# Bias rows stored sixteen times in memory, each copy shifted by one number more, and read back at multiples of 64 bytes

## The chip, the cores and the metric

The kernel runs on one core of one Trainium2 chip (trn2). The metric is device time in microseconds (us) of one execution. Before the change three runs took 1264.16 us in the median (1261.74 to 1264.27).

## What is computed

One inference step of a two-layer decoder for a prompt of 256 tokens and 8 samples of one token each (model width 1024, 16 heads of 64). Layer 0 is attention in three groups g, with windows 128, 512, 2048 and dilations 1, 4, 16; layer 1 is a pooling mixer; each is followed by a mixture of experts (16 experts, two per token). Everything is float32. What matters for the change is the relative bias of the prompt's attention:

```
step = BAND + qi - kj                               # distance of query and key
bias = bias_tab[t5_bucket(max(step, 0) * dilation)] # (query, key, head)
sc = q . k * HEAD_DIM ** -0.5 + bias
sc = where(step in window, sc, -1e30); p = softmax(sc)
```

The bias depends on the distance alone. So for a head and a group it is one row of numbers by distance, and the 128 queries of a block need that row at 128 successive offsets. The three groups are merged by a softmax over their log sums, and attention also hands back keys and values; the caches of the samples are copied to the outputs, shifted by one token (168 copies of 1 MB, called `move` in the code).

## The kernel before, in words

The five instruction streams (PE, DVE, ACT, POOL, SP) are written out by hand and meet at semaphores. SP issues nearly all large DMAs, in one fixed order on one queue (q1): weights and caches for the matmuls, with copies of the sample caches (`move`, L342) put between them as filling. ACT's own DMAs go to a second queue (q10), POOL's to a third (q0). All queues are served by the same 16 DMA engines.

**Start.** x is transposed on PE (L1035), its squares are summed (L287), and ACT takes the root (L294). At the same time PE makes the bias rows: a table of 33 x 48 numbers times 0/1 rows by distance (L1041) gives 16 heads x 384 distances for each group, and DVE copies them to `bias_rows` on 16 partitions (L771). ACT then stores them to the tensor `bias_by_distance` in HBM (L612), issues six DMAs for constants (L613 to L618), and waits until the store has landed (L619), because the memory of `bias_rows` is used again in the next stage. SP, which has issued three chunks of w_qkv (2 MB each) and five copies of the first cache, waits for the same store (L352) and then issues seven more copies. POOL waits for it ahead of its first broadcast (L483).

**w_qkv.** 72 tiles of 128 columns: PE multiplies (L1059), ACT squares the result (L626), PE sums squares (L1066), ACT takes the root (L632), DVE its reciprocal and the product (L787, L788), POOL keeps the tile (L492). PE runs at most two tiles ahead of the first square. SP loads chunks of four tiles into three slots; the chunk for tiles 12 to 15 is issued when four tiles are done.

**Samples.** The samples' attention over the caches: scores on DVE beside the tiles, then PE's products with V (L1103, L1110, L1103), whose V loads come in two halves of three loads of 2 MB (L376). Ahead of the second half SP issues the bias loads of heads 0 to 3 (`bias_load`, L367), and five copies.

**Prompt attention.** 16 heads, one step per head. PE makes the scores (L1127, L1130), DVE adds the bias from `bias_t` and takes the maximum (L846, L849, L851), ACT takes exponentials (L670, L672), DVE scales (L862, L863), PE transposes (L1138) and multiplies with V (L1145, L1150). `bias_t` has four slots of 128 x 3 x 256 numbers; when head h has been biased (`biased`), SP loads the slot for head h + 4 (L367) and issues one copy. A load is one DMA: partition p reads, for each group, 256 numbers from the row of its head beginning at number p, so its 384 pieces of 1 KB begin at multiples of 4 bytes.

After that come w_o (L1171), two mixtures of experts with the pooling layer between them, and the transposes of the result.

Of the kernel before, what the change touches and what calls it, by code (L numbers as in the profile page):

```python
# [7 lines left out]
F32 = mybir.dt.float32  # L8
# [4 lines left out]
P = 128  # L13
# [30 lines left out]
def build(nc, x_prompt, x_sample, cache_w128, cache_w512, cache_w2048, state_pool, w_qkv, q_norm,  # L44
# [4 lines left out]
    _, SEQ, D = x_prompt.shape  # L49
# [3 lines left out]
    G = len(WINDOWS)  # L53
    NB, GH = rel_bias.shape
    H = GH // G
# [10 lines left out]
    BV = 3 * P  # L66
# [13 lines left out]


    qkvs_dram = nc.dram_tensor("qkv_of_samples", [NS, 3, G, D], F32, kind="Internal").ap()
    bias_dram = nc.dram_tensor("bias_by_distance", [H, G, BV], F32, kind="Internal").ap()

    with ExitStack() as ctx:
        def sb(name, shape):
# [61 lines left out]
        bias_rows = cut(7680, (G, BV))  # L148
# [176 lines left out]
        def _(sp):  # L325
# [23 lines left out]
            sp.wait_ge(buckets_landed, 32)  # L349
            for b in range(5):  # L350
                move(0, b, 0)
            sp.wait_ge(bias_stored, 16)  # L352
            for b in range(5, NS):
                move(0, b, 0)
            for n in range(PIECES[1]):
# [8 lines left out]

            def bias_load(h, b):

                sp.dma_start(bias_t[:, b], bass.AP(tensor=bias_dram.tensor, offset=h * (G * BV),  # L367
                                                   ap=[[1, P], [BV, G], [1, SEQ]])).then_inc(bias_landed[b], 16)

            for half in range(2):  # L370
                for g in range(G):
# [97 lines left out]
        def _(pool):  # L469
            pool.dma_start(pool_s[0, :, 0:STATE - 1, :].rearrange("b s c -> b (s c)"),  # L470
                           state_pool[0, :, 1:STATE, :].rearrange("b s c -> b (s c)")).then_inc(tokens_sent, 16)
            for g in range(G):
                def load_k(b):
                    pool.dma_start(slot(3)[:, b % 4 * D:(b % 4 + 1) * D], k_strided[g][b]).then_inc(k_landed[b % 4], 16)

                def spread_q(b):
                    at = 32 * (b // 3 + 1)

                    if b % 2 == 0 and b <= 2:
                        pool.wait_ge(zn_kept, g * NQK + (NQK - 2 + b))  # L480
                    if b >= 1:
                        pool.wait_ge(q_spread, g * NS + b)
                    pool.wait_ge(bias_stored, 16)  # L483
                    nc.gpsimd.partition_broadcast(q_rep[b % 2][:, :], q_row[at:at + 1, b % 3, :], channels=P).then_inc(q_spread, 1)  # L484

                for b in range(4):
                    load_k(b)
                for n in range(NQK):
                    pool.wait_ge(zn_ready, g * NZ + n + 1)
                    if n == KT + 6:  # L490
                        pool.wait_ge(q_spread, g * NS + 2)
                    nc.gpsimd.tensor_copy(qk[:, g, n // KT, n % KT, :], zn[:, n % 4, :]).then_inc(zn_kept, 1)  # L492
                    if n == KT + 3:
                        pool.wait_ge(z_stored, g * NZ + KT)
                        for at in range(0, NS, 3):
                            n_rows = min(3, NS - at)
                            pool.dma_start(q_row[32 * (at // 3 + 1):32 * (at // 3 + 1) + 1, 0:n_rows, :],
                                           qkv_s[at:at + n_rows, 0, :]).then_inc(q_rows_landed, 16)
                        pool.dma_start(qkvs_dram[:, 0, g], qkv_s[0:NS, 0, :]).then_inc(q_sent, 16)
                    if n == KT + 5:  # L500
                        pool.wait_ge(q_rows_landed, g * 48 + 48)
                        for b in range(2):
                            spread_q(b)
                for b in range(NS):
                    pool.wait_ge(scored, g * NS + b + 1)
                    if b + 2 < NS:
                        spread_q(b + 2)
                    if b + 4 < NS:
                        load_k(b + 4)
                pool.wait_ge(z_stored, (g + 1) * NZ)  # L510
                pool.dma_start(qkvs_dram[:, 1:3, g], qkv_s[0:NS, 1:3, :]).then_inc(rows_sent, 16)
                dst = kv_p[g][0, 0].rearrange("t w h e -> t w (h e)")
                if g == 0:
                    pool.dma_start(dst[:, 0, :], k_tok[1]).then_inc(tokens_sent, 16)
                    for a in range(2):
                        pool.dma_start(dst[a * HD:(a + 1) * HD, 1, :], v_tok[a * HD:(a + 1) * HD, 1, g, :]).then_inc(tokens_sent, 16)
                else:
                    for b in range(2):
                        pool.dma_start(dst[b * P:(b + 1) * P, 0, :], k_tok[b]).then_inc(tokens_sent, 16)
                    pool.dma_start(dst[:, 1, :].rearrange("(b p) c -> p b c", p=P), v_tok[:, :, g, :]).then_inc(tokens_sent, 16)  # L520
                pool.wait_ge(rows_sent, g * 16 + 16)
                pool.dma_start(kv_s[g][0, :, kv_s[g].shape[2] - 1].rearrange("b w h e -> b w (h e)"),
                               qkv_s[0:NS, 1:3, :]).then_inc(tokens_sent, 16)
# [73 lines left out]
        def _(ac):  # L597
            dma = ac.dma_start
# [10 lines left out]
            ac.wait_ge(setup_done, 1)  # L609
            norm_root(ac, 0, h_filled, KT)  # L610
            ac.wait_ge(bias_copied, 1)
            dma(bias_dram.rearrange("h g d -> h g d"), bias_rows[0:H, :, :]).then_inc(bias_stored, 16)  # L612
            dma(bucket_s[:], c_bucket_sample.rearrange("g n k -> n g k")).then_inc(consts_landed, 16)  # L613
            dma(same_batch[:], c_same_batch).then_inc(consts_landed, 16)
            dma(rank[:], c_rank[:, 0:NE]).then_inc(consts_landed, 16)
            dma(slot_no[:], c_rank[:, NE:NE + CAP]).then_inc(consts_landed, 16)
            dma(same_head[:], c_rank[:, NE + CAP:]).then_inc(consts_landed, 16)
            dma(tri[:], c_tri).then_inc(consts_landed, 16)  # L618
            ac.wait_ge(bias_stored, 16)  # L619


            with ac.Fori(0, G) as g:
# [124 lines left out]
        def _(dve):  # L747
# [90 lines left out]
            def step(i, s, live, behind):  # L838
                h = i * 4 + s
                b = s % 2  # L840
                if live:
                    dve.wait_ge(scores_ready, h + 1)
                    dve.wait_ge(bias_landed[s], i * 16 + 16)
                    c = 8 * b
                    vec.memset(small[:, 60:61], 0.0)
                    vec.tensor_tensor_reduce(out=probs[:, b, 0:G * P].rearrange("p (g k) -> p g k", g=G), in0=bank[0][:, 0:G * P].rearrange("p (g k) -> p g k", g=G),  # L846
                                             in1=bias_t[:, s, :, P:], scale=1.0, scalar=NEG, op0=ALU.add, op1=ALU.max,
                                             accum_out=small[:, 16 + c:17 + c])
                    vec.tensor_tensor_reduce(out=probs[:, b, 3 * P:7 * P], in0=bank[1][:, :], in1=bias_t[:, s, 0:2, :].rearrange("p g k -> p (g k)"),  # L849
                                             scale=1.0, scalar=NEG, op0=ALU.add, op1=ALU.max, accum_out=small[:, 17 + c:18 + c])  # L850
                    chain(vec.tensor_tensor_reduce(out=probs[:, b, 7 * P:], in0=bank[2][:, 0:SEQ], in1=bias_t[:, s, 2, :],  # L851
                                                   scale=1.0, scalar=NEG, op0=ALU.add, op1=ALU.max, accum_out=small[:, 18 + c:19 + c]))
                    vec.tensor_scalar(small[:, c + 3:c + 4], small[:, 16 + c:17 + c], -1.0, None, ALU.mult)
                    vec.tensor_scalar(small[:, c + 2:c + 3], small[:, 17 + c:18 + c], small[:, 18 + c:19 + c], -1.0,
                                      ALU.max, ALU.mult).then_inc(biased, 1)
# [529 lines left out]
```

## Time and profile before

| | before |
|---|---|
| median of 3 runs | 1264.16 us |
| profiled execution, its own time | 1266.1 us |
| its span, first to last instruction | 1263.9 us |
| mean granted TensorE clock | 0.922 of full |
| PE busy | 1113.8 us (88%) |
| DVE / ACT / POOL busy | 435.8 / 234.0 / 225.0 us |
| DMA packets, bytes | 62930, 462.63 MB, mean 366 GB/s |

The page and the views are of one profiled execution. Times are us from the start of the span, and a duration without a unit is in us. PE is the matmul unit (PEld its weight loads), DVE the vector engine, ACT the scalar engine, POOL the GpSimd; SPq, ACTq and POOLq are instructions that only issue DMAs. In a timeline a row is start, duration, engine, line, operation, out<-in and count; the idle time before it and what ended it stand in brackets. For DMA issues the last number is the time from issue to landing, the median where there are several. PEclk is the clock that TensorE was granted, as a share of 2.4 GHz.

### The profile page before, as it was taken

What the parts mean: (1) busy time and instruction counts of PE and PEld (TensorE: products, weight loads), DVE (VectorE), ACT (ScalarE), POOL (GpSimd) and SP (SyncE); (2) the same over time, 40 slices, a digit from 0 to 9 for tenths busy, and PEclk for the clock granted to TensorE, in tenths of its full rate; (3) what the DMA queues carried; (4) which work ended last, traced back from release to release, by engine and by line L of the source; (5) the groups of instructions that cost most, each with busy time, mean ns of one, the idle gap of its engine ahead of it and who ended that gap; (6) DMA issues with size and microseconds to landing.
All of it is one profiled execution on the core that took longest, in us unless ns stands there. A gap on an engine that the chain in (4) does not pass through costs nothing.

```text
span 1263.9 us, 15314 instructions
## 1 busy us (share of the span) xinstructions
PE 1113.8 (88%) x4993; PEld 671.7 (53%) x4994; DVE 435.8 (34%) x859; ACT 234.0 (19%) x524; POOL 225.0 (18%) x484
## 2 busy tenths in 40 slices
PE   5998799999949899974979999999464999999998
PEld 3887588788822588863424444434343344334444
DVE  3456455845830366223101111111743111111113
ACT  1121122112110134211112122111101112112210
POOL 1014112411420122002122222110001122222210
PEclk9999899999967699985989999999665999999999
DMA  9999999999879998899999999999999899999996
GB/s 374 334 357 372 385 387 343 369 389 388 322 239 384 368 308 288 344 320 326 330 399 429 430 427 413 400 399 394 399 325 322 327 396 397 398 395 396 409 420 241
DMA packets 62930, 462.63 MB, mean 366 GB/s; under 512 B 12112, under 2 KB 20192, under 8 KB 47888
## 3 DMA queue, kind: packets, MB, share of 16 engines
q1 hardware_dynamic: 49136, 440.29, 90.8%
q0 software_dynamic: 5536, 18.88, 4.1%
q10 hardware_dynamic: 8232, 3.13, 1.1%
q8 instruction: 14, 0.23, 0.1%
q14 instruction: 12, 0.10, 0.0%
HBM read 455.19 MB, written 183.41 MB: 505 GB/s over the span
## 4 chain that ended last, share of the span: by engine, by line
PE 56%; DVE 8%; DMA 4%; issue 3%; POOL 1%; ACT 1%; ACTq 1%; POOLq 0%; DVEq 0%; SPq 0%
PE bank L1242 17%; PE bank L1264 8%; PE bank L1220 7%; PE bank L1209 5%; DMA region_a<-in_w_up_dram 3%; PE bank L1171 2%; PE bank L1103 2%; PE bank L1130 1%; PE bank L287 1%; PE bank L1138 1%; PE bank L1150 1%; PE bank L1181 1%; PE bank L1270 1%; PE bank L1110 1%; PE bank L1127 1%
## 5 line engine op out<-in xcount | busy, mean ns | idle before, releaser
L1059 PE MATMUL bank<-uT,ring_lo 128*128 128x264 f32 x1152 | 276.0, 394 | 8.5 <-DVE uT L300 6.0
L1059 PEld LDWEIGHTS bank<-uT,ring_lo 128*128 128x128 f32 x1152 | 219.5, 195 | 49.4 <-issue 9.7
L1242 PE MATMUL bank<-ring_lo,scratch 128*64 128x512 f32 x512 | 114.7, 601 | 16.0 <-DMA ring_lo<-in_w_gate_dram 8.0
L787 DVE RECIPROCAL scratch<-scratch 128x264 f32<-128x264 f32 x48 | 86.5, 1802 | 111.0 <-ACT scratch L632 111.0
L1220 PE MATMUL bank<-scratch 128*128 128x512 f32 (+1 forms) x192 | 99.7, 646 | 18.0 <-POOL scratch L570 18.0
L1264 PE MATMUL bank<-ring_lo,scratch 128*64 128x512 f32 x512 | 113.4, 595 | 1.3 <-issue 1.3
L1242 PE MATMUL bank<-region_a,scratch 128*64 128x512 f32 x512 | 112.7, 592 | 1.4 <-DMA region_a<-in_w_up_dram 1.4
L966 DVE TENSOR_TENSOR scratch<-bank,scratch 128x512 f32<-128x512 f32 x16 | 11.1, 691 | 228.5 <-PE bank L1242 228.5
L1209 PE MATMUL bank<-scratch 128*128 128x264 f32 x288 | 80.1, 404 | 4.4 <-DVE scratch L966 3.4
L555 POOL TENSOR_TENSOR small<-epsc 128x1 f32<-128x1 f32 x83 | 15.6, 193 | 378.7 <-PE bank L1270 359.9
L1242 PEld LDWEIGHTS bank<-ring_lo,scratch 128*64 128x64 f32 x512 | 36.8, 138 | 83.6 <-issue 75.4
L1242 PEld LDWEIGHTS bank<-region_a,scratch 128*64 128x64 f32 x512 | 38.3, 137 | 73.2 <-issue 73.2
L1264 PEld LDWEIGHTS bank<-ring_lo,scratch 128*64 128x64 f32 x512 | 35.8, 137 | 70.4 <-issue 70.4
L1209 PEld LDWEIGHTS bank<-scratch 128*128 128x128 f32 x288 | 49.5, 190 | 41.4 <-issue 25.1
L1220 PEld LDWEIGHTS bank<-scratch 128*128 128x128 f32 (+1 forms) x192 | 32.2, 194 | 72.7 <-issue 54.2
L956 DVE TENSOR_TENSOR hT<-bank,hT 128x264 f32<-128x264 f32 x144 | 60.5, 429 | 26.0 <-PE bank L1209 24.9
L960 DVE COPY scratch<-bank 128x512 f32<-128x512 f32 x16 | 11.1, 691 | 169.0 <-PE bank L1220 169.0
L492 POOL COPY region_a<-scratch 128x264 f32<-128x264 f32 x48 | 24.4, 508 | 193.2 <-DVE scratch L788 192.8
L578 POOL TENSOR_SCALAR scratch<-slot_no,scratch 128x64 f32<-128x64 f32 (+1 forms) x96 | 53.4, 574 | 0.0
L626 ACT ACTIVATE scratch<-bank 128x264 f32<-128x264 f32 x48 | 18.8, 391 | 159.7 <-PE bank L1059 159.7
L798 DVE TENSOR_TENSOR ring_lo<-ring_lo,scratch 128x1024 f32<-128x1024 f32 x24 | 41.7, 1738 | 16.6 <-POOL scratch L484 9.9
L738 ACT ACTIVATE scratch<-bank 128x512 f32<-128x512 f32 x32 | 19.1, 597 | 126.6 <-PE bank L1264 126.6
(224 smaller groups left out, 1242.4 us busy)
## 6 DMA issues: line engine op xcount, KB each, us to landing
out_dram<-in_cache_kv_w_dram SPq DMA_DIRECT2D x128, 1023.5 KB, 18.8
ring_lo<-in_w_gate_dram SPq DMA_DIRECT2D x32, 2048.0 KB, 12.0
region_a<-in_w_up_dram SPq DMA_DIRECT2D x32, 2048.0 KB, 15.2
ring_lo<-in_w_down_dram SPq DMA_DIRECT2D x32, 2048.0 KB, 16.5
ring_lo<-in_w_qkv_dram SPq DMA_DIRECT2D x18, 2048.0 KB, 18.0
out_dram<-in_cache_kv_w_dram SPq DMA_DIRECT2D x32, 1022.0 KB, 35.9
ring_lo<-in_cache_kv_w_dram POOLq DMA_DIRECT2D x24, 512.0 KB, 11.8
ring_lo<-in_cache_kv_w_dram SPq DMA_DIRECT2D x6, 2048.0 KB, 14.7
```

Source lines behind the costliest of these rows:

```text
L492: nc.gpsimd.tensor_copy(qk[:, g, n // KT, n % KT, :], zn[:, n % 4, :]).then_inc(zn_kept, 1)
L578: last = nc.gpsimd.tensor_scalar(pick_gate[0:n, b, at], slot_no[0:n, :], pair_at[0:n, 0, b, e:e + 1], pair_at[0:n, 1, b, e:e + 1], ALU.is_ ...
L787: chain(vec.reciprocal(zri[:, n % 2, :], zr[:, n % 2, :]))
L798: chain(vec.tensor_tensor(k_tile, k_tile, q_rep[b % 2][:, :], ALU.mult))
L956: vec.tensor_tensor(hT[:, m, :], spread_bank[m % 4][:, 0:T], hT[:, m, :], ALU.add).then_inc(spread_added, 1)
L1059: last = mm(z_bank[s % 4][:, 0:T], w[:, k, at:at + P], uT[:, k, :], start=(k == 0), stop=(k == KT - 1))
L1103: last = mm(bank[3 + a][rows, :], p_masked[:, b % 2, g, rows], slot(g)[:, at:at + 512], start=(half == 0 and g == 0 and b % 2 == 0), stop= ...
L1171: last = mm(bank[m % 2][:, 0:T], w[:, f % 4, m * P:(m + 1) * P], oT[:, f, :], start=(f == 0), stop=(f == KT - 1))
L1209: mm(spread_bank[m % 4][:, 0:T], y_pair[:, m * P:(m + 1) * P], place, start=True, stop=True).then_inc(spread, 1)
L1220: last = mm(bank[a][:, :], pick[0:sizes[b], b, :], u_tok[0:sizes[b], b, a * 512:(a + 1) * 512], start=(b == 0), stop=(b == 2))
L1242: last = mm(bank[2 + w][rows, :], u_slots[:, k, rows], weights[e][w][:, k, :], start=(k == 0), stop=(k == KT - 1))
L1264: last = mm(bank[4 + a][rows, :], hid[:, f, rows], weights[e][2][:, f, a * 512:(a + 1) * 512], start=(f == 0), stop=(f == FT - 1))
```

## The change

`bias_by_distance` holds each head's rows 16 times. Copy s begins at distance index s, and a row has 384 - 16 = 368 numbers (1472 bytes, a multiple of 64). The store is 16 DMAs, one per copy, and each wait for it now asks for all 16. A load for one head is three DMAs, one per group: partition p = 16 a + s reads from copy s, beginning at number 16 a, which gives the same 256 numbers as before, from an address that is a multiple of 64 bytes. DVE waits for three landings where it waited for one.

```diff
-    bias_dram = nc.dram_tensor("bias_by_distance", [H, G, BV], F32, kind="Internal").ap()
+    SHIFTS = 16
+    BL = BV - SHIFTS
+    bias_dram = nc.dram_tensor("bias_by_distance", [H, SHIFTS, G, BL], F32, kind="Internal").ap()
...
-            sp.wait_ge(bias_stored, 16)
+            sp.wait_ge(bias_stored, 16 * SHIFTS)
...
-                sp.dma_start(bias_t[:, b], bass.AP(tensor=bias_dram.tensor, offset=h * (G * BV),
-                                                   ap=[[1, P], [BV, G], [1, SEQ]])).then_inc(bias_landed[b], 16)
+                for g in range(G):
+                    sp.dma_start(bias_t[:, b, g, :], bass.AP(tensor=bias_dram.tensor, offset=h * (SHIFTS * G * BL) + g * BL,
+                                                             ap=[[SHIFTS, P // SHIFTS], [G * BL, SHIFTS], [1, SEQ]])).then_inc(bias_landed[b], 16)
...
-                    pool.wait_ge(bias_stored, 16)
+                    pool.wait_ge(bias_stored, 16 * SHIFTS)
...
-            dma(bias_dram.rearrange("h g d -> h g d"), bias_rows[0:H, :, :]).then_inc(bias_stored, 16)
+            for s in range(SHIFTS):
+                dma(bias_dram[:, s], bias_rows[0:H, :, s:s + BL]).then_inc(bias_stored, 16)
...
-            ac.wait_ge(bias_stored, 16)
+            ac.wait_ge(bias_stored, 16 * SHIFTS)
...
-                    dve.wait_ge(bias_landed[s], i * 16 + 16)
+                    dve.wait_ge(bias_landed[s], i * (16 * G) + 16 * G)
```

## Rows read from the trace of the kernel before

**Rows 1.** Page: busy us (share) x instructions; chain by engine.

```profile
PE 1113.8 (88%) x4993; PEld 671.7 (53%) x4994; DVE 435.8 (34%) x859; ACT 234.0 (19%) x524; POOL 225.0 (18%) x484
...
PE 56%; DVE 8%; DMA 4%; issue 3%; POOL 1%; ACT 1%; ACTq 1%; POOLq 0%; DVEq 0%; SPq 0%
```

**Rows 2.** Timeline of PE, 20 to 48 us: start, us, engine line op [idle before].

```profile
30.27 9.95 PE L1059 MATMUL bank<-uT,ring_lo 128*128 128x264 f32 x32 [6.03 <-DVE uT L300]
40.06 0.61 PE L1066 MATMUL bank<-scratch,blockones 128*128 128x264 f32 x2
```

**Rows 3.** Timeline of ACT, 24 to 45 us.

```profile
24.28 0.34 ACTq L612 DMA_DIRECT2D bias_by_distance<-scratch  x1
...
27.15 0.45 ACTq L618 DMA_DIRECT2D tri<-in_c_tri_dram  x1
36.70 0.39 ACT L626 ACTIVATE scratch<-bank 128x264 f32<-128x264 f32 x1 [11.94 <-PE bank L1059]
```

**Rows 4.** DMA issues on ACT's queue: count, KB each, us to landing.

```profile
bias_by_distance<-scratch ACTq DMA_DIRECT2D x1, 72.0 KB, 4.6
...
bucket_s<-in_c_bucket_sample_dram ACTq DMA_DIRECT2D x1, 48.4 KB, 5.8
...
same_batch<-in_c_same_batch_dram ACTq DMA_DIRECT2D x1, 4.0 KB, 9.6
rank<-in_c_rank_dram ACTq DMA_DIRECT2D x1, 8.0 KB, 21.2
```

**Rows 5.** Stretches: us, busy per engine (x), PEclk, DMA share, GB/s.

```profile
24.20:28.20 4.00, 0.04 (x1) 0.00 (x0) 3.31 (x5) 0.48 (x1) 0.00 (x0) 1.00 1.06 390
28.97:35.80 6.83, 5.54 (x13) 4.38 (x14) 1.13 (x4) 0.00 (x0) 0.00 (x0) 0.52 1.05 405
```

**Rows 6.** SP's queue: timeline, and landing of the fifth copy.

```profile
1.73 15.38 SPq L348 DMA_DIRECT2D ring_lo<-in_w_qkv_dram  x3
...
24.34 0.59 SPq L342 DMA_DIRECT2D out_dram<-in_cache_kv_w_dram  x1
...
out_dram<-in_cache_kv_w_dram SPq DMA_DIRECT2D x1, 1016.0 KB, 22.4
```

**Rows 7.** DMA queues, 29.3 to 50 us: packets, MB, share of 16 engines.

```profile
q1 hardware_dynamic: 410, 7.42, 102.7%
q10 hardware_dynamic: 410, 0.05, 1.7%
```

**Rows 8.** Stretches in and after the prompt attention, columns of rows 5.

```profile
447.40:452.80 5.40, 5.40 (x41) 4.59 (x40) 3.90 (x14) 2.10 (x7) 2.95 (x4) 1.00 0.95 322
540.00:549.00 9.00, 9.00 (x42) 7.57 (x40) 0.86 (x2) 0.00 (x0) 0.00 (x0) 1.00 0.74 168
```

**Rows 9.** PE and DVE near 445 us, and DVE's waits from 415 to 520.

```profile
443.86 1.46 PE L1130 MATMUL bank<-scratch 64*128 64x256 f32 x6
...
445.36 0.55 DVE L846 CUSTOM_DVE_ANT_1 scratch<-bank,ring_lo 128x384 f32<-128x384 f32 x1 [2.36 <-issue]
...
DVE scratch L846 <- issue: 14.6, 13, 4.3
```

**Rows 10.** SP's first bias load in the loop; its landing.

```profile
427.90 0.40 SPq L367 DMA_DIRECT2D ring_lo<-bias_by_distance  x1
...
ring_lo<-bias_by_distance SPq DMA_DIRECT2D x1, 384.0 KB, 14.3
```

**Rows 11.** SP and PE around the V loads; packets from 371.5 to 378 us.

```profile
370.53 1.96 SPq L367 DMA_DIRECT2D ring_lo<-bias_by_distance  x4
...
383.27 7.35 SPq L376 DMA_DIRECT2D ring_lo<-in_cache_kv_w_dram  x3
...
ring_lo<-in_cache_kv_w_dram SPq DMA_DIRECT2D x1, 2048.0 KB, 16.9
...
403.86 14.14 PE L1103 MATMUL bank<-ring_lo,scratch 128*32 128x512 f32 x48
...
DMA packets 1615, 2.56 MB, mean 393 GB/s; under 512 B 64, under 2 KB 1600, under 8 KB 1600
```

## The prediction

> **What bounds the kernel now.** I read the page first. PE is busy for 88% of the span, and the chain that ended last is mostly PE [rows 1]; the 16 DMA engines are busy nearly throughout, but a stage is only bound by them where PE waits for a landing. So I looked at the two places that the diff touches, each for what ends last there.
>
> The first is the start. PE turns x and sums squares until 24.2, is idle for 6.03 us, runs the first two tiles of w_qkv from 30.27 (32 records, 9.95 us), and then needs the squares of tile 0 (L626, on ACT) for L1066 at 40.06 [rows 2]. ACT issues the store of the bias rows at 24.28 and six constants, the last at 27.15, then waits for the store, and is next busy at 36.70 with L626, for tile 0's z [rows 3]. The store had landed 4.6 us after its issue, at 28.9 [rows 4]. So ACT could leave its wait up to 40.06 - 0.39 = 39.67 and PE would lose nothing: the store has 10.8 us of slack. Everything behind it, 24 tiles in each of three groups, hangs on this chain.
>
> The second is the prompt attention, 422 to 515, one head in 5.4 us. PE is busy 5.40 of 5.40 us there [rows 8], and DVE's add of the bias starts 0.04 us after the last score matmul (443.86 + 1.46 = 445.32 to 445.36) [rows 9]. DVE's idle time ahead of that line, 14.6 us in 13 pieces, is marked "issue", which could hide a wait for the bias [rows 9]; but the load for head 4 was issued at 427.90 and took 14.3 us, so it was there at 442.2, 3.2 us before it was used [rows 10], and the loads after it have a lead of three heads, 16 us. The reads are not what this stage waits for.
>
> **The change, part by part.**
>
> *The store.* One DMA of 16 rows becomes 16 DMAs of 16 x 3 pieces of 1472 B, 1.13 MB in all. Issues on ACT follow each other at (27.15 - 24.28) / 6 = 0.48 us [rows 3], so 15 more take 15 x 0.48 = 7.2 us, and the last store is issued at 31.5. If it landed as the one of before did, 4.6 us later, the wait would end at 36.1, still 3.6 us inside the slack: cost nothing. The six constants move 7.2 us back, to 34.8; they are used only after all 72 tiles.
>
> But it won't land like that, and the trace shows why. On SP's queue lie five copies of a cache, 1016 KB each in 16 pieces of 65 KB, the fifth issued at 24.34, behind the rest of w_qkv [rows 6]. From 29.3 to 50 SP's queue (q1) ran 410 packets with 7.42 MB and ACT's queue (q10) 410 packets with 0.05 MB [rows 7]: the DMA engines take one packet of each in turn, and a packet of q10 stands behind a copy's piece. The 8 small packets per engine of same_batch and rank landed 9.6 and 21.2 us after issue where bucket_s, ahead of the copies, took 5.8 [rows 4]. rank was issued one place, 0.5 us, behind same_batch, so its 128 rows (8 per engine and a completion) came 12.1 us after same_batch's, which is 1.35 us a packet. The 16 stores are 3 pieces and a completion per engine each, 64 packets. They begin to move at about 28, when the engines are turning to the copies; at 1.35 us a packet 64 would take 86 us. That is no real end, because SP waits for the same semaphore (L352) before it issues copies 6 to 12: behind the fifth copy q1 is empty, and the rest of the stores then run freely. The fifth copy landed 22.4 us after 24.34, at 46.7 [rows 6]. All the stores' bytes at the 390 GB/s of that stretch [rows 5] are 1.13 / 0.39 = 2.9 us, most of it spent ahead of or between the copies on some engines and behind them on others. Bounds for the end of the wait: 36.1 (stores slip ahead) and 46.7 + 2.9 + 4.6 = 54.2 (all run behind the copies with a full landing). I take 46.7 + 1.8 = 48.5, nearest to the fifth copy's row, since some engine always has stores left at that point.
>
> What waits behind: ACT's L626, then PE's L1066, DVE's reciprocal and POOL's copies, so the whole chain. L626 ends at 48.9, and L1066 starts there instead of at 40.06: **+8.8 us** (bounds 0 and 54.6 - 40.1 = 14.5). ACT has then two tiles waiting and catches up within tile 2.
>
> *TensorE's clock.* PE is idle for 8.8 us, 40.2 to 49. After its 6.03 us idle at 24.2 the granted clock was 0.52 of full from 28.97 to 35.80 (the 1.2 GHz level for nearly all of it) [rows 5], and tile 0 took 30.27 to 36.70, 6.4 us, where tile 1 took the rest of the 9.95, 3.5 [rows 2, 3]. So I add what that cost, 6.4 - 3.5 = **+2.9 us** (bounds 0 and half of 6.83, 3.4).
>
> *SP.* Its copies 6 to 12 are issued from 48.5 instead of 28.9. The w_qkv chunk for tile 12 is issued when four tiles are done, at about 59 now, behind 7 copies that at 390 GB/s take 7 x 2.7 = 19 us from 48.5, and is needed 8 tiles of 3.5 us or more later, at 87: nothing. POOL's wait for the store (L483) comes after twelve tiles: nothing. The DMA idle time that this leaves is made up before anything waits for a copy: SP's queue runs dry again in 540 to 549 (168 GB/s [rows 8]).
>
> *The reads.* Each load becomes three DMAs of 128 rows of 1 KB, the same 384 pieces. SP issues one in 0.39 us [rows 10], so two more are 0.8 us of a head's 5.4 us, in which SP mostly waits: hidden. The first four loads put 8 x 0.5 = 4 us ahead of five copies; SP's issue of the four ended at 372.5, and its next V load was issued at 383.27 [rows 11], after a wait for PE that was longer than that: hidden. What a read at a multiple of 64 B saves cannot be told from the trace, as there is none. From below: the first four loads, 1.57 MB, moved in 6.4 us (371.6 to 378.0 [rows 11]), 1.6 us a load; were half of that saved, it would be 0.8 us a head in a stage with 3.2 us and more of lead. From above: it costs up to the double, see the third rival. I take **0**.
>
> The Trainium skill speaks against a gain too: by "DMA: Bandwidth & Descriptors", section "How a descriptor splits into AXI transactions", a read begins at the 256 B boundary below its start, in beats of 32 B. By that a 1 KB row costs 32 beats and, averaged over starts at multiples of 4 B, 4.4 more, and over multiples of 64 B 3 more, an estimate of 4% less for the reads; no run here shows it, and the sum would be the same.
>
> **Sum.** 8.8 + 2.9 + 0 = +11.7 us. Against the profiled execution (1266.1 us, its span 1263.9 and 2.2 around it) that is 1277.8; this execution lies 1.9 above the median of the runs, so I forecast 1264.2 + 11.7 = **1275.9 us**.
>
> **Rivals.**
> 1. *The stores slip ahead; no change.* If an engine takes several small packets to one large, or most stores run before the copies begin, the wait ends by 39.7 and the time is 1264. For: the free sum ends at 36.1, and at 24.3 SP's copies are still queued behind w_qkv. Against: 410 to 410 packets [rows 7]. Chance 10%.
> 2. *Faster: the aligned reads pay.* If the 14.6 us ahead of L846 [rows 9] were waits for the bias and not for the scores, loads twice as fast would take back up to 14.6 - 4.3 (the first, at the 1.2 GHz level) = 10.3 us in the attention; it decides only if loads land after their scores, and with rival 1 beside it (or a store that costs under 10) it gives 1254 to 1262. Against: 442.2 against 445.36. Chance 5%.
> 3. *The reads use half the DMA engines; slower still.* The source of a load now begins with a count of 8 (8 x 16 x 256) where it had 128. If a transfer is dealt by that count over 8 engines, the first four loads take 6.4 x 2 = 12.8 us on these, and V's three loads of the second half come up to 6.4 us later: the first landed at 383.27 + 16.9 = 400.2 for PE's need at 403.86 [rows 11], so +2.7 us. In the loop such an engine would have 3.2 us of bias and 2.7 us of copy per head, 5.9 us in place of 5.4; over 12 heads 6 us behind, against a lead of 3.2 to 10 us: 0 to 3 us. Together +3 to +6 on top: 1279 to 1282. Whether it costs depends on the lead of 3.7 us being used up. Chance that it is seen in the time: 15%.
> The Trainium skill has such a rule: "DMA: Bandwidth & Descriptors", section "Why a DMA increments its semaphore by 16 and not by 1", takes the largest number up to 16 that divides both slowest dimensions, which is 8 for this source. By that rule the load is dealt over 8 engines; no transfer of the trace of before has such a source. I hold the dealing likely, its price mostly hidden.
> 4. *ACT's stores are short of queue room, so that the issue itself blocks*, as for SP's three w_qkv chunks (15.38 us to issue [rows 6]). The constants would then be issued at the end, 6 x 0.48 = 2.9 us after 48.5: 1278.8. Chance 8%.
>
> **How the numbers follow.** The forecast's mechanism holds 62% (1270 to 1280, by the wait's end at 44 to 52 and a clock loss of 0 to 3.4); rivals 3 and 4 lie above or at its edge with 23%, rival 1 and 2 below with 15%. A measurement of this kernel tells about 0.2%, 2.5 us. The range leaves out rival 2, most of rival 1, and the far end of 3: 1266 to 1281. Slower 0.84, same 0.11, faster 0.05.
>
> **What would show it.** In the profile after: ACT's first L626 at about 48.5 with the bias store as what it waited for, L1066 at 49, PE idle for 8 to 9 us before it, granted clock half after it; the same 5.4 us per head and no more idle time ahead of L846; and from 60 on all stages as before, 11 us later. Wrong if L626 still starts at 36.7, if the stores' landing is spread over more than the five copies, or if the attention's length moves by over 2 us.

## The result and the profile after

The changed kernel takes 1276.18 us in the median of four runs (1275.58 to 1277.49), the kernel before, in the same session and now also in four runs, 1264.22 (1261.74 to 1264.92): a ratio of 1.0100, with an interval of 1.0082 to 1.0117. It is slower by 12.0 us; 11.7 had been forecast. The profiled execution took 1276.4 us (span 1274.2), 10.3 more than the one before, which lay 1.9 above its median. Late in the file a line number is 4 higher than before.

The page of the changed kernel: busy time, packets, the queues (packets, MB, share of 16 engines).

```profile
PE 1117.7 (88%) x4993; PEld 675.4 (53%) x4994; DVE 436.6 (34%) x859; ACT 234.1 (18%) x524; POOL 225.4 (18%) x484
...
DMA packets 64050, 463.68 MB, mean 364 GB/s; under 512 B 12480, under 2 KB 21328, under 8 KB 49008
...
q10 hardware_dynamic: 9224, 4.19, 1.5%
```

No engine has more to do, against [rows 1]: PE's 3.9 us more busy time are fewer than the 10.3 lost. So time is lost in waits, and the start has the first. ACT's timeline of the changed kernel, where [rows 3] stood:

```profile
25.97 7.93 ACTq L616 DMA_DIRECT2D bias_by_distance<-scratch  x16
...
34.89 4.63 ACTq L619 DMA_DIRECT2D rank<-in_c_rank_dram  x1
39.54 6.05 ACTq L620 DMA_DIRECT2D slot_no<-in_c_rank_dram  x1
45.62 3.71 ACTq L621 DMA_DIRECT2D same_head<-in_c_rank_dram  x1
49.36 0.46 ACTq L622 DMA_DIRECT2D tri<-in_c_tri_dram  x1
50.98 0.67 ACT L630 ACTIVATE scratch<-bank 128x264 f32<-128x264 f32 x2 [24.54 <-DMA bias_by_distance<-scratch]
```

PE's timeline beside it, where [rows 2] stood:

```profile
31.96 8.91 PE L1063 MATMUL bank<-uT,ring_lo 128*128 128x264 f32 x32 [6.03 <-DVE uT L302]
51.43 1.25 PE L1070 MATMUL bank<-scratch,blockones 128*128 128x264 f32 x2 [10.56 <-ACT scratch L630]
52.47 5.26 PE L1063 MATMUL bank<-uT,ring_lo 128*128 128x264 f32 x16
...
58.01 3.72 PE L1063 MATMUL bank<-uT,ring_lo 128*128 128x264 f32 x16
```

ACT's first square waits for the 16 stores until 50.98 (forecast 48.5), PE is idle for 10.56 us, and its next tile of 16 matmuls takes 5.26 us where the one after takes 3.72. Two things beside it were not in the sum. This execution was 1.7 us late before the stores even began (the first w_qkv matmul at 31.96, 30.27 before). And three constants took 4.6, 6.1 and 3.7 us to *issue*, where their neighbours took 0.45: rival 4 happened in part, for the constants but not for the stores (16 in 7.93 us). It cost nothing, since ACT was through at 49.82, ahead of the stores' last landing.

The queues of the changed kernel from 29.3 to 50 us, where [rows 7] stood, and the stores' median landing:

```profile
q1 hardware_dynamic: 278, 4.92, 63.0%
q10 hardware_dynamic: 1409, 1.19, 31.2%
...
bias_by_distance<-scratch ACTq DMA_DIRECT2D x10, 69.0 KB, 16.0
```

SP's queue moves 4.92 MB in place of 7.42 and then has nothing left, because SP itself stands at the same wait; a store lands after 16 us instead of 4.6. The end of the stretch shows something that the prediction had not. The fifth copy, issued at 23.96, its landing, then ACT's queue from 44 to 50.8, then SP's next copies:

```profile
out_dram<-in_cache_kv_w_dram SPq DMA_DIRECT2D x1, 1016.0 KB, 21.9
...
q10 hardware_dynamic: 1328, 0.77, 75.9%
...
50.80 1.77 SPq L344 DMA_DIRECT2D out_dram<-in_cache_kv_w_dram  x3
```

The last copy landed at 45.9, and the stores still took 4.9 us more, with ACT's queue (these and the constants) keeping the engines 75.9% busy at 113 GB/s. The prediction had let them "run freely" at 390 GB/s there and be done in 1.8.

Where the two executions stand to each other, by the start of the same instruction (square: ACT L626, now L630):

| place | before | after | later by |
|---|---|---|---|
| first w_qkv matmul | 30.3 | 32.0 | 1.7 |
| square of tile 2 | 44.3 | 57.8 | 13.5 |
| last square ahead of group 1 (tile 15) | 98.5 | 112.0 | 13.5 |
| next square (group 1) | 152.8 | 159.5 | 6.7 |
| last square | 319.0 | 326.7 | 7.7 |
| first product with V | 375.6 | 385.6 | 10.0 |
| first score of the prompt | 421.6 | 432.6 | 11.0 |
| first matmul of w_o | 520.5 | 532.6 | 12.1 |
| end | 1263.9 | 1274.2 | 10.3 |

Half of the 13.5 us is given back at the end of group 0, and some is lost again later. The give-back first. DVE's waits in the kernel before from 98 to 160 us (engine, what, releaser: us, times, longest), and POOL's four K loads of that stretch (count, KB each, median us to landing):

```profile
DVE ring_lo L798 <- DMA ring_lo<-in_cache_kv_w_dram: 6.4, 1, 6.4
...
ring_lo<-in_cache_kv_w_dram POOLq DMA_DIRECT2D x4, 512.0 KB, 13.1
```

The same four loads in the changed kernel; there the line of the wait is gone:

```profile
ring_lo<-in_cache_kv_w_dram POOLq DMA_DIRECT2D x4, 512.0 KB, 6.3
```

Before, samples' scores waited 6.4 us for their keys (the K wait below), behind SP's copies and w_qkv chunks: SP's queue took 99.5% of the engines from 115 to 126. After, PE and with it everything that issues loads in step stands still while the copies run on, and the keys find free engines: SP's queue takes 31.5% from 130 to 142. How much this gives varies. From the square of tile 2 to group 1's it is 108.6 us in the execution of before shown here and 101.7 in the changed kernel, 6.9 less. In four kernels below whose time equals that of before, the wait is 3.7, 2.0, 6.0 and 5.1 us and the stretch 104.6, 102.7, 106.3 and 105.5. Against those the give-back is 1.0 to 4.6.

### The profile page after: what moved, and what is told of

It is laid out like the page before. It is cut to its first block, busy times and chain, and to the rows that moved or that the text cites. A ratio compares the mean times of both kernels' runs of the same rounds, so it can differ in the third digit from the quotient of the medians.

```text
span 1274.2 us, 15409 instructions
## 1 busy us (share of the span) xinstructions
PE 1117.7 (88%) x4993; PEld 675.4 (53%) x4994; DVE 436.6 (34%) x859; ACT 234.1 (18%) x524; POOL 225.4 (18%) x484
## 4 chain that ended last, share of the span: by engine, by line
PE 56%; DVE 8%; DMA 4%; issue 3%; POOL 1%; ACT 1%; ACTq 1%; POOLq 0%; DVEq 0%; SPq 0%
PE bank L1246 17%; PE bank L1268 8%; PE bank L1224 7%; PE bank L1213 5%; DMA region_a<-in_w_up_dram 3%; PE bank L1107 2%; PE bank L1175 2%; PE bank L1134 1%; PE bank L1154 1%; PE bank L289 1%; PE bank L1142 1%; PE bank L1185 1%; PE bank L1274 1%; PE bank L1114 1%; PE bank L1131 1%
## 5 line engine op out<-in xcount | busy, mean ns | idle before, releaser
L1063 PE MATMUL bank<-uT,ring_lo 128*128 128x264 f32 x1152 | 275.7, 394 | 8.6 <-DVE uT L302 6.0
L1063 PEld LDWEIGHTS bank<-uT,ring_lo 128*128 128x128 f32 x1152 | 219.4, 195 | 49.6 <-issue 9.6
L1224 PE MATMUL bank<-scratch 128*128 128x512 f32 (+1 forms) x192 | 99.1, 643 | 18.1 <-POOL scratch L573 18.1
L630 ACT ACTIVATE scratch<-bank 128x264 f32<-128x264 f32 x48 | 18.7, 391 | 168.4 <-PE bank L1063 143.8
L802 DVE TENSOR_TENSOR ring_lo<-ring_lo,scratch 128x1024 f32<-128x1024 f32 x24 | 41.8, 1740 | 14.8 <-POOL scratch L487 14.5
```

The lines of the kernel that those rows point to most:

```text
L802: chain(vec.tensor_tensor(k_tile, k_tile, q_rep[b % 2][:, :], ALU.mult))
L1063: last = mm(z_bank[s % 4][:, 0:T], w[:, k, at:at + P], uT[:, k, :], start=(k == 0), stop=(k == KT - 1))
L1224: last = mm(bank[a][:, :], pick[0:sizes[b], b, :], u_tok[0:sizes[b], b, a * 512:(a + 1) * 512], start=(b == 0), stop=(b == 2))
```

## The experiments

Each ratio is to the kernel before, run in the same session on the same chip (its medians: 1262.61 for the first four, 1261.07 for two copies ahead and the three without effect, 1260.40 for the last four).

### Stores alone

The 16 stores are made, but the reads are those of before, from an unshifted tensor that takes the place of copy 0 in the store.

```diff
...
-            for s in range(SHIFTS):
+            dma(bias_whole.rearrange("h g d -> h g d"), bias_rows[0:H, :, :]).then_inc(bias_stored, 16)
+            for s in range(1, SHIFTS):
                 dma(bias_dram[:, s], bias_rows[0:H, :, s:s + BL]).then_inc(bias_stored, 16)
...
```

> The sixteen stores alone: one store of the whole rows and fifteen of the shifted ones (which nobody reads), every wait for all sixteen, and the loads as before: one DMA per head from the whole rows, at multiples of 4 bytes. Theory (the store's wait behind SP's five copies is the cost): L626's counterpart starts near 51 as in the changed kernel, and the time is 1273 to 1278. Rival (the reads over half the DMA engines cost it): 1263 to 1266.

1270.65 us (1269.04 to 1271.91), ratio 1.0057 (1.0040 to 1.0074), which is 7.2 us (5.1 to 9.3). ACT's timeline of this kernel:

```profile
50.35 0.67 ACT L631 ACTIVATE scratch<-bank 128x264 f32<-128x264 f32 x2 [24.23 <-DMA bias_by_distance<-scratch]
```

The square of tile 2 is 13.0 us later than before, group 1's 7.0 and the end 5.8. The stores alone make the start's loss, the give-back and over half of the 12 us.

### Three loads in place of one

The kernel before with each bias load split by group, from unaligned addresses.

```diff
-                sp.dma_start(bias_t[:, b], bass.AP(tensor=bias_dram.tensor, offset=h * (G * BV),
-                                                   ap=[[1, P], [BV, G], [1, SEQ]])).then_inc(bias_landed[b], 16)
+                for g in range(G):
+                    sp.dma_start(bias_t[:, b, g, :], bass.AP(tensor=bias_dram.tensor, offset=h * (G * BV) + g * BV,
+                                                             ap=[[1, P], [1, SEQ]])).then_inc(bias_landed[b], 16)
...
```

> The other half alone: one store as before, but each load is three DMAs, one per group, still of 128 rows that begin at multiples of 4 bytes. Theory: SP issues three in some 1.5 us where it had one in 0.4, all of it hidden: 1262 to 1266, attention (first score matmul to first of w_o) within 1 us of the 98.9 before. Rival (issue and completions of three DMAs cost the attention): 1266 to 1270.

1260.34 us (1258.44 to 1265.44), ratio 0.9993 (0.9978 to 1.0009): two more issues and waits a head cost nothing.

### No copy ahead of the wait, in both kernels

The changed kernel, and the one before, with SP's five copies moved behind its wait for the store.

```diff
-            for b in range(5):
-                move(0, b, 0)
             sp.wait_ge(bias_stored, 16 * SHIFTS)
-            for b in range(5, NS):
+            for b in range(0, NS):
```

> The changed kernel with SP's first five copies issued behind its wait for the stores instead of ahead of it. Theory: nothing large stands beside the stores once w_qkv has landed (near 32), so the wait ends soon after the last store's issue, 36 to 40, PE stalls by 0 to 1 us, and the time is 1258 to 1268 (what the groups' K loads meet changes too, by up to 7 us). Rival (sixteen stores are slow by themselves, or ACT's queue has no room): the wait still ends past 46 and the time stays at 1273 to 1278.

> The kernel before with the same five copies issued behind the wait: the control of the last one. Theory: the one store is not late in either order, so the first squares start at 36.7 as before; only the phase of the copies against the K loads of the samples moves: 1257 to 1266. Rival (copies held back cost by themselves): 1267 or more.

The changed kernel: 1271.94 us (1268.60 to 1279.55), ratio 1.0085 (1.0057 to 1.0113). The one before: 1265.18 (1260.67 to 1268.28), ratio 1.0023 (1.0007 to 1.0038). The changed kernel's ACT, then its SP:

```profile
25.08 11.15 ACTq L614 DMA_DIRECT2D bias_by_distance<-scratch  x16
...
39.89 0.67 ACT L628 ACTIVATE scratch<-bank 128x264 f32<-128x264 f32 x2 [14.34 <-DMA bias_by_distance<-scratch]
```

```profile
39.23 8.49 SPq L344 DMA_DIRECT2D out_dram<-in_cache_kv_w_dram  x12
48.80 0.40 SPq L360 DMA_DIRECT2D ring_lo<-in_w_qkv_dram  x1
49.46 27.47 SPq L344 DMA_DIRECT2D out_dram<-in_cache_kv_w_dram  x3
77.24 0.40 SPq L360 DMA_DIRECT2D ring_lo<-in_w_qkv_dram  x1
```

and its waits from 60 to 115 us:

```profile
PE bank L1061 <- DMA ring_lo<-in_w_qkv_dram: 3.3, 1, 3.3
...
DVE ring_lo L800 <- DMA ring_lo<-in_cache_kv_w_dram: 7.6, 1, 7.6
```

The mechanism of the start is shown: without the copies the wait ends at 39.9, where the prediction had put the slack's end (39.67), and the square of tile 2 is 0.4 us from where it was. But the stores are also slow by themselves. With nothing beside them, from 32 to 38 us, this kernel's DMA shows:

```profile
DMA packets 519, 0.58 MB, mean 96 GB/s; under 512 B 128, under 2 KB 519, under 8 KB 519
...
q10 hardware_dynamic: 519, 0.58, 91.5%
```

The 16 engines are 91.5% busy in the mean and move 96 GB/s, a quarter of the 390 that the prediction took for them, which it had read where w_qkv was loaded. From the first store's issue to SP's next instruction it is 14.2 us (25.08 to 39.23) against 24.8 in the changed kernel (25.97 to 50.80), so the five copies are 10.7 us of the wait and the stores themselves the rest. Why they are so slow isn't shown; no run changed how a store is laid out.

My expected time was missed all the same. Twelve copies that start at 39 stand ahead of the w_qkv chunks (SP hangs 27 us in the issue of three copies, and the next chunk goes out at 77), PE waits 3.3 us for one, tile 15 is 5.5 us late, the K wait is 7.6 us, and group 1 begins 6.4 us late. Moving the copies costs something without the 16 stores too: the control is 0.23% or 2.9 us above the kernel before. The stall at the start was not the only price of bytes on that stretch of the queue: taken away there, the work that must go through before the keys comes up 60 us further on.

### Two copies ahead

The changed kernel with 2 of the 12 copies ahead of the wait in place of 5.

```diff
-            for b in range(5):
+            for b in range(2):
                 move(0, b, 0)
             sp.wait_ge(bias_stored, 16 * SHIFTS)
-            for b in range(5, NS):
+            for b in range(2, NS):
```

> The changed kernel with two of SP's five copies ahead of its wait for the stores and three behind it: the dose between the changed kernel (five, wait ends at 50.8) and the one with none (39.8). Theory (the wait ends when the queued copies have drained and the stores run free): each copy is worth some 2.7 us, or nothing while ACT is still issuing, so the wait ends between 40 and 45, and tile 2's square (44.3 in the kernel before) comes at 45 to 51. What the time makes of it depends on the transfers behind: 1262 to 1274. Rival (the number of copies doesn't matter once one is there): the wait ends near 50.

1271.56 us (1270.90 to 1273.28), ratio 1.0084 (1.0068 to 1.0101). Its ACT:

```profile
25.54 14.55 ACTq L616 DMA_DIRECT2D bias_by_distance<-scratch  x16
...
43.69 0.67 ACT L630 ACTIVATE scratch<-bank 128x264 f32<-128x264 f32 x2 [17.68 <-DMA bias_by_distance<-scratch]
```

With 0, 2 and 5 copies ahead the wait ends at 39.9, 43.7 and 51.0: 2.2 us a copy. The K wait is 7.7 us, and group 1 begins 6.3 us late, though the start lost only 5.9. All four kernels with 16 stores arrive at group 1 at 159.2 to 159.8, whether the start lost 0.4, 5.9, 13.0 or 13.5 us: in the two with fewer copies ahead, what was saved at the start was gone again before group 1. Why the four agree so closely isn't shown.

### Eight copies, at two alignments

The changed kernel with eight shifts. Rows of 376 numbers give pieces at multiples of 32 bytes, rows of 377 at multiples of 4 only. Both sources now begin with a count of 16.

```diff
-    SHIFTS = 16
+    SHIFTS = 8
...
-    BL = BV - SHIFTS        # in the second kernel alone
+    BL = BV - SHIFTS + 1
```

> The changed kernel with 8 shifted copies instead of 16: 8 stores, and a load's source is 16 x 8 x 256, first count 16, at multiples of 32 bytes. Theory (dealing by the first count of a source that can't be merged): the first four loads run at a DMA share near 1 and over 300 GB/s where the changed kernel had 0.5 and 190; the stores' wait still ends behind the five copies, 47 to 50, since 8 stores are 32 packets per engine against 10 of the copies; time 1268 to 1275. Rival (half the stores, half the delay): wait ends near 43, 1264 to 1268.

> The last kernel with rows of 377 numbers instead of 376, so that the same loads from the same 8 copies begin at multiples of 4 bytes only. It isolates what the multiple itself is worth. Theory: nothing, the first four loads take the same time within 0.5 us and the times are equal within 2 us. Rival (alignment makes the reads faster): the first four loads take 1 us or more longer and their pieces' share is higher.

Multiples of 32 bytes: 1267.65 us (1264.59 to 1269.21), ratio 1.0058 (1.0039 to 1.0076). Multiples of 4: 1268.32 (1266.78 to 1271.29), ratio 1.0067 (1.0045 to 1.0088). The wait ends at 46.42 with the first, the square of tile 2 is 8.7 us late, and there is no K wait: group 1 begins 1.6 us late. The first bias loads, SP's queue over 4 us in the middle of them (packets, MB, share of 16 engines), in the kernel before (372 to 376):

```profile
q1 hardware_dynamic: 1027, 1.02, 100.0%
```

the changed kernel (384 to 388), and SP's issue of the 12 loads:

```profile
q1 hardware_dynamic: 735, 0.71, 52.7%
...
379.89 7.78 SPq L370 DMA_DIRECT2D ring_lo<-bias_by_distance  x12
```

eight shifts at 32 bytes (376 to 380), then at 4 bytes (378.2 to 382.2):

```profile
q1 hardware_dynamic: 919, 0.84, 81.6%
```

```profile
q1 hardware_dynamic: 881, 0.80, 75.0%
```

Share times 16 engines times 4 us over the packets gives the mean time of a packet on its engine, the few bytes of a completion counted as one too: 62 ns before, 46 in the changed kernel, 57 and 54 with eight shifts. The three loads at 4 bytes from one stored row, above, took 55 (1031 packets at 88.1%, from 367 to 371). Between 32 and 4 bytes there is no gain, neither in the packet nor in the time. The changed kernel's packet is shorter by a quarter, but half the engines carry it: 0.71 MB in 4 us in place of 1.02. Whether the 46 ns come from the alignment or from fewer engines at work isn't told apart: no run had 64-byte pieces on 16 engines.

That 8 engines carry the changed kernel's loads and 16 these shows a second way, too. The trace holds 108 increments of each slot's semaphore for its 12 loads in the changed kernel, 9 a load (one for each engine and one more), and 192, 16 a load, with eight shifts and in the three-loads kernel. But I had expected over 300 GB/s and the wait's end at 47 to 50, and got 211 and 46.4; the time, 1267.65, came out just below the 1268 to 1275 that I had named. SP took 8.69 us to issue these 12 loads of 1.57 MB (5.57 in the three-loads kernel), which is 181 GB/s, so the issue may be what held them; no run separates it.

### Three attempts without effect

Three edits of the kernel before that should have put the loads on eight engines, or cut the copies' pieces.

```diff
-                sp.dma_start(bias_t[:, b], bass.AP(... ap=[[1, P], [BV, G], [1, SEQ]])).then_inc(bias_landed[b], 16)
+                    sp.dma_start(bias_t[:, b, g, :], bass.AP(... ap=[[16, P // 16], [1, 16], [1, SEQ]])).then_inc(bias_landed[b], 16)
...
-[:, at:at + m].rearrange("b (n x y) -> b n x y", n=n, x=16)
+[:, at:at + m].rearrange("b (n x y) -> b n x y", n=n, x=128)    # third kernel: x=64
```

> The kernel before with three DMAs per load (as in the three-loads experiment) and the source written as 8 x 16 x 256 with steps 16, 1, 1: the same bytes from the one stored row, at multiples of 4 bytes, but its first count is 8. Theory (a transfer is dealt by that count over 8 DMA engines): while the first four loads run alone the DMA share is about 0.5 and some 190 GB/s, as in the changed kernel, and the pieces take longer where 8 engines read one row; time 1260 to 1266, V loads up to 3 us later. Rival (the dealing comes from the aligned copies' layout, not from the count): share 0.8 to 1.0 as before.

> The kernel before with every copy of a sample cache cut in 128 pieces of 8 KB instead of 16 of 65 KB. Theory (queues take turns by packet, so small packets stand behind a copy's piece): rank lands within 8 us of its issue instead of 21.2, K loads in 6 to 8 us instead of 11.8 at the median, and DVE's wait for a K load (6.4 us near 128) is gone: 1252 to 1260. Rival (SP's queue has less room for copies of 128 pieces, so SP is held up and the weights come late): 1264 to 1285.

> The kernel before with every copy cut in 64 pieces of 16 KB. Theory: as with 8 KB, half as strong: K loads land in 7 to 10 us at the median, the 6.4 us wait shrinks to under 2: 1255 to 1262. Rival (room in SP's queue): 1264 to 1280, less than with 8 KB.

1259.90 us (ratio 0.9982 to 1.0006), 1261.62 (0.9990 to 1.0017) and 1260.36 (0.9984 to 1.0003). None did what it was meant to. The first one's loads ran at 93% of 16 engines (1.00 MB in 4 us), which lies in the range that its rival had named. I read it otherwise: 8 x 16 rows with steps of 16 and 1 are 128 rows with a step of 1 and seem to be merged to that, since with eight shifts the count of 16 did bring 16 engines. The other two have the 62930 packets and 462.63 MB of before: writing the contiguous copy as 64 or 128 pieces did not change how it was cut. They serve as repeats of before (spans 1256.7 and 1257.5) and as the K waits given above.

### Copies in pieces of 8 KB

The kernel before with the copies' source and target written so that rows can't be joined.

```diff
-[:, at:at + m].rearrange("b (n x y) -> b n x y", n=n, x=16)
+[:, at:at + m].rearrange("b (n z x y) -> b n x z y", n=n, z=8, x=16)
```

> The kernel before with the cache copies really cut in pieces of 8 KB: the pieces are listed in an order that can't be merged (16 outer with step 8 KB, 8 inner), since in the two earlier tries the packets stayed those of before. Theory (queues take turns by packet): rank lands under 10 us after issue instead of 21, K loads in 5 to 9 us at the median instead of 11.8, the DVE's wait for a K load is under 1 us: 1254 to 1260 where before is 1261. Rival (8 KB pieces copy slower, or SP's queue has less room): 1262 to 1280.

1430.73 us in the median of four runs (1398.44 to 1460.20). The ratio of the two shortest, 1398.44 and 1416.21, is 1.1161 (1.1076 to 1.1246). Its profiled execution is the longest of the four, so only its DMAs are read here. Issues from 24 to 60 us, and ACT's timeline later:

```profile
slot_no<-in_c_rank_dram ACTq DMA_DIRECT2D x1, 32.0 KB, 14.6
...
rank<-in_c_rank_dram ACTq DMA_DIRECT2D x1, 8.0 KB, 11.8
```

```profile
593.16 50.16 ACTq L703 DMA_DIRECT2D region_a<-in_pool_w_dram  x1
643.35 91.65 ACTq L705 DMA_DIRECT2D region_a<-in_c_inv_count_dram  x4
```

The small loads at the start land sooner, rank after 11.8 us in place of 21.2 [rows 4]: as a shorter turn behind a shorter piece would have it. But later ACT is held for 142 us in five issues. Why shorter pieces make that worse I can't say from these rows; it stays open.

### Seven copies moved behind the attention

The kernel before with copies 6 to 12 taken from the start and issued ahead of w_o's wait, to take away the bytes that make the K wait.

```diff
             sp.wait_ge(bias_stored, 16)
-            for b in range(5, NS):
-                move(0, b, 0)
-            for n in range(PIECES[1]):
-                move(1, 0, n)
...
+            for b in range(5, NS):
+                move(0, b, 0)
+            for n in range(PIECES[1]):
+                move(1, 0, n)
```

> The kernel before with the seven copies that follow the wait for the store (the last three of the first cache and four of the second) issued just ahead of the wait for w_o instead. Theory (in the changed kernel these copies ran while PE stood still, which is what took the K load's wait of 6.4 us away in group 0): that wait is gone or under 1 us, and group 0 ends 4 to 7 us earlier; what the copies cost later (19 us of DMA in front of w_down and the copies behind it) may take part of it back: 1255 to 1264. Rival (the wait does not hang on the backlog): it stays at 5 to 7 us.

1356.16 us (1353.15 to 1357.68), ratio 1.0749 (1.0724 to 1.0773). The expected time is missed by far. At its start the expected happens: the K wait is gone and group 1 begins 4.7 us earlier, 102.4 us after tile 2's square where it was 108.6 (and 102.7 to 106.3 in the four kernels like before). Then its ACT and its PE:

```profile
520.15 73.16 ACTq L697 DMA_DIRECT2D wr<-in_router_group_w_dram  x1
593.34 52.91 ACTq L698 DMA_DIRECT2D wr<-in_router_expert_w_dram  x1
...
654.36 5.87 PE L287 MATMUL bank<-scratch,ones 128*128 128x264 f32 x16 [106.25 <-ACT scratch L292]
```

and its queues from 560 to 640 us:

```profile
q1 hardware_dynamic: 1001, 27.49, 96.9%
q10 hardware_dynamic: 1057, 0.04, 0.8%
```

ACT's timeline of the kernel before, same loads:

```profile
521.13 17.11 ACTq L697 DMA_DIRECT2D wr<-in_router_group_w_dram  x1
538.26 3.44 ACTq L698 DMA_DIRECT2D wr<-in_router_expert_w_dram  x1
```

and its queues from 538 to 542 us, where SP's runs dry:

```profile
q10 hardware_dynamic: 2781, 0.09, 42.7%
q1 hardware_dynamic: 18, 0.07, 4.6%
```

It is the queues' turns again, at another place and eight times the price: 1001 packets to 1057, one packet of SP's queue per small packet. 80 us x 16 / 1001 = 1.28 us a turn in the mean, long pieces and short completions together. The router's weights go in small packets: in the kernel before, 2781 packets of ACT's queue pass in these 4 us, here 1057 in 80. ACT stands inside the issue, so PE waits 106 us for its next work (2.5 before).

## Why the prediction was right, and where by luck

**Right, and shown.** The store is what the start waits for, and SP's five copies are what makes it late: the kernel with the stores alone has the same wait, and with fewer copies ahead it ends earlier, 2.2 us a copy. Packets of the two queues take turns where both have work, 410 to 410 before.

**Right in size by luck: "46.7 + 1.8".** "I take 48.5" met 50.8 at SP and 50.98 at ACT. Both terms were off. The fifth copy landed at 45.9, not 46.7, and what was left of the stores took 4.9 us, not 1.8: they don't run at 390 GB/s but at 113 (96 in the kernel without copies). The "free sum" of 36.1, 11.8 us from the first issue, was short too: without copies it took 14.2, so the 16 stores would have used up nearly all of the slack with no copy beside them. How much of the 2.5 us is this execution's late start of the stores (25.97 against 24.28) isn't shown.

**Right in kind: the clock.** Its step is in the changed kernel's stretch from L1070 to the next L1063 but one (columns of rows 5):

```profile
51.43:58.01 6.58, 6.58 (x21) 5.29 (x21) 2.30 (x2) 0.95 (x3) 0.40 (x1) 0.69 0.98 348
```

Before, the same work from 40.06 to 44.51 took 4.45 us at a granted clock of 1.00. At 0.69 it took 2.1 more; "+2.9" had been said.

**Wrong: "nothing" for SP.** The start lost 13.5, not 11.7 (1.7 of it had come before the stores), and then 6.9 came back in a place where the prediction said that nothing waits. It had asked whether a delayed copy would be late for w_qkv, and not what the delay would free. A wait for keys of 6.4 us was in the kernel before (2.0 to 6.0 in its four likes), and no row for it was read. The runs show both halves: with 8.7 us or more lost at the start (four kernels) there is no such wait; with 5.9 or less it is 2.0 to 7.7 us; and with the seven copies gone it is gone too.

**Nearly right: "0" for the reads.** They are dealt over half the engines, as rival 3 had it (52.7% share, 182 GB/s for 255). By the Trainium skill, "DMA: Bandwidth & Descriptors", section "Why a DMA increments its semaphore by 16 and not by 1", a source that begins with 8 gets 8 engines; the trace agrees (52.7%, and 9 increments a load). Its price wasn't rival 3's +3 to +6 as worked out: the attention took 100.0 us in place of 98.9, and SP's three issues for a head (2.37 us at 438.89, 0.40 before) were hidden. The V loads of the second half went out at 393.19, 9.9 us later than before with everything 10.0 later, and PE took their product at 413.87 without a pause.

**Left open.** The medians say +12.0 for the change and +7.2 or 8.0 for the stores alone (ratio or medians; separate sessions, and their intervals, 10.4 to 14.8 and 5.1 to 9.3, don't touch). The split loads alone cost nothing. So 4 to 5 us are left that would be the shifted reads', but the traces don't show them there. The two profiled executions end 4.5 us apart (spans 1274.2 and 1269.7) though they reach the last square together (326.7). Of these 4.5 us, 2.5 come between the last square and the first product with V, ahead of the first bias load and so not by the reads (DVE waits 4.2 us for POOL's broadcasts there, 2.4 before); 0.9 come in the attention (100.0 against 99.1) and 1.1 after it. What the reads cost beyond the attention's 1 us stays open.

So the forecast's 0.3 us from the median is in part luck: two terms of the wait that were off against each other, a start 1.8 us worse, a give-back of 1 to 7 that was not seen, and 4 to 5 us of loss that were not in the sum.

No kernel here beats the one before; the four within its noise are three that don't do what they should and the split loads.

## What to carry to other kernels

A small DMA that somebody waits for takes turns with the bulk queue, here 1.28 to 1.35 us a packet, so count its packets per engine before multiplying it, not its bytes. Take the rate of what is left from a row of the same kind of transfer: these stores ran at a quarter of the rate that loads had shown. When a stall is added or removed early, look downstream for the waits that it feeds or starves: here between none and 7 us of the start's loss came back before the next stage, and removing most of the stall won nothing that shows in the time. Before paying for an alignment, check what it gives and whether the pieces still spread over all the engines: 32 bytes gave nothing here, and the layout for 64 halved the engines.

## What was not expected of the hardware

- An issue can hold its engine: 4.6, 6.1 and 3.7 us for constants of 8 to 32 KB, 27.5 for three copies, 73.2 for one 16 KB load behind the copies (0.4 to 0.5 for an issue that isn't held). That the queue has no room then is my reading; the trace shows the time alone. The prediction read the dry spell of SP's queue from 540 to 549 [rows 8] as slack; moving seven copies took it away and cost 106 us of PE's time, because ACT's router loads get through just there.
- 16 stores of 69 KB, each from 16 partitions in pieces of 1472 B, move at 96 GB/s with the 16 engines 91.5% busy and nothing beside them.
- The turns between queues are one packet each: 410 to 410, 1001 to 1057. The Trainium skill, same page, section "Queues, rings and completion order", says that an engine drains a whole packet of some 9 to 17 descriptors from a queue before it switches; the rows agree that queues take turns, but with one record of the profile from each queue, not 9 to 17.
- Pieces of 1 KB at multiples of 32 bytes are no faster than at multiples of 4 (57 and 54 ns a packet).
